# Page numbers loaded four at a time, and reductions, gates, one weight tile and the first weighings moved within their engines' lists, in a one-core decoder step

## The chip, the cores and the metric

The kernel runs on one core of a Trainium2 chip. The metric is the device time of one execution in microseconds (us). Less is better.

## What is computed

One inference step of one decoder layer, for a prompt of 1024 tokens and for eight single new tokens ("samples") with stored state. Four mixers read the same normed input through one input projection `w_in`; their gated outputs go through one output projection. Cut to what matters here:

```python
h = rms_norm(x, norm_pre); proj = h @ w_in              # 1024 x 7688 columns
# A: causal pooling over windows of 2, 4, 8, 16
# B: mLSTM, 4 heads of 128:   num = (q k^T * w_intra) v + (q C) * w_inter
#    C_new = w_old * C + sum_s w_s k_s v_s^T ;  h = num / max(|den|, exp(-m))
# C: stick-breaking attention, 8 heads of 64, strictly causal:
#    A[t,s] = sigmoid(z_ts) * prod_{s<j<t} (1 - sigmoid(z_tj)),  out = A v
#    a sample attends to 4096 stored tokens: 32 pages of 128, by page_table
k_past = cache_sb_k[page_table]; v_past = cache_sb_v[page_table]
# D: softmax cross-attention, 4 heads, into 256 memory tokens
out = rms_norm(concat(A, B, C, D) * gates @ w_out, norm_post); y = x + out
```

## The kernel before

Every engine has its own list, written out by hand; semaphores tie them together, and an engine that waits holds up all that stands behind it in its list. There are five stages, and a stage starts when all engines have left the one before: the first (norm, transposes, memory keys and values, first projections; to about 95 us), stick-breaking (to 500), mLSTM (to 825), memory attention and pooling (to 1134), output projection.

TensorE (PE) multiplies everything. The projections of w_in are done in column tiles of 128: a tile is loaded by SyncE (SP), split into a high half by ScalarE (ACT, `w_hi`) and a low half by VectorE (DVE, `w_lo`), and multiplied in 3 chunks of 24 matmuls (line 417 in the first two stages, line 163 later). A chunk needs both halves. Two tiles' halves are held at a time.

The samples' part of C runs beside this. The 4096 stored tokens are handled in 16 pairs of pages per sample. For keys: SP loads two page numbers into registers (`value_load`, line 2225), waits until the ring of 4 pairs has room (`z_ready`: the pair four before has been reduced) and issues two DMAs (line 2229); GpSimd (POOL) multiplies the pair by the query (line 2237); DVE reduces it to scores (`reduce_keys`, line 2243). After 16 pairs come `add_bias`, a softplus on ACT and DVE (`softplus`, line 2267), a sum on PE (`sum_pages`, line 2275), `exponents` and the weights. For values: SP loads two page numbers and issues two DMAs (lines 2353, 2357) when PE has weighed the pair four before, and PE weighs two pairs at a time (`weigh`, line 2370). Samples 0 to 3 have their keys in the first two stages and their values in stick-breaking; samples 4 to 7 have their keys in mLSTM (one per head) and their values in the memory stage.

Stick-breaking goes in 4 passes `i` of two heads each (called heads here), each of 12 rounds `u`, counted from 0 (HALF is round 4). In a round PE computes scores, one projection chunk, transposes the weights of two rounds ago and weighs the values of three rounds ago (line 1153). DVE does in a round: scans (lines 990, 994), products (line 1003), where due `open_gate`, `split_lo` (line 396), `exponents`, and then `reduce_keys(i + 1, REDUCES[i][u])`. `gate(i, 0)` (line 1010) multiplies the first half of the outputs by the gate; PE's weighing in round 7 writes the same bank and waits for it (`y_taken`). It stands at the start of round 7, behind the reductions of round 6. In the first head `REDUCES[0]` puts the first two reductions of sample 1 in round 2, ahead of `softplus(0)` of sample 0, for which `sum_pages(0)` on PE waits in round 3. SP's list in the first head (lines 814 to 849) has, in this order: key pairs 4 to 8, the values' store, key pair 9, the fourth projection tile (for rounds 9 to 11, split in round 6), key pairs 10 and 11, value pairs 4 and 5, and so on.

mLSTM has four heads with five tiles each: K, V, Q, O, G. In each head SP loads 4 key pairs, then Q, 3 key pairs, the stored C, then O (lines 1783 to 1795). PE multiplies V, transposes K, multiplies Q's first chunk, transposes V (`turn_values`: it needs DVE's `b_kw_tok`, and that needs ACT's `b_w_col`, which stands behind ACT's split of O), then Q's other chunks; `spread_values` (line 2105) waits for DVE's eight updates of C (line 1965).

## Time and profile before

| | |
|---|---|
| median of 3 runs | 1342.79 us (1336.55 to 1345.03) |
| the profiled execution | 1344.1 us; its span 1342.4 us |
| PE busy | 1227.8 us, 91% of the span |
| DVE, ACT, POOL busy | 832.4, 472.1, 388.2 us |
| granted TensorE clock, mean | 0.961 of full speed |
| DMA | 235.80 MB, 176 GB/s on average |

The page gives busy times per engine, the span in 40 slices, the chain of work that ended last and the costliest groups of instructions. A wait is shown as idle time of an engine with what ended it. "SPq" is SyncE's queue, whose register and DMA-issuing instructions are not counted as busy.

### The profile page before, as it was taken

The numbers are of one execution on the slowest core, as the hardware profiler recorded it, in microseconds if no ns is written. First come the engines' busy times: TensorE is split into PE (matmuls) and PEld (weight loads), VectorE is DVE, ScalarE is ACT, GpSimd is POOL, SyncE is SP. The second block draws the span as 40 slices with busy tenths as digits, with TensorE's granted clock in tenths as the row PEclk, the third lists the DMA queues.
The fourth block names the chain that finished last, engine by engine and source line by source line (L and its number), as shares of the span: only waits on it lengthen the run. The fifth ranks groups of instructions, "written<-read, shape, count | busy, mean of one in ns | idle before, by whom it ended". The sixth has DMA issues, their size and how long they took to land.

```text
span 1342.4 us, 22563 instructions
## 1 busy us (share of the span) xinstructions
PE 1227.8 (91%) x7621; PEld 1027.2 (77%) x7621; DVE 832.4 (62%) x1096; ACT 472.1 (35%) x873; POOL 388.2 (29%) x261
## 2 busy tenths in 40 slices
PE   5896989989989986899999999799999998999997
PEld 5885757768768666799998998587888876568886
DVE  5758987999974544779798696343543344433221
ACT  6524535545545741132321324312222132322211
POOL 2476534433530015547664562000000000000000
PEclk9998989999999987899998999899999998999999
DMA  8776488587583446466555542856556654645220
GB/s 287 231 221 189 125 255 248 165 244 226 164 261 105 137 90 212 142 199 203 184 173 181 168 152 87 265 178 196 170 178 203 192 173 141 204 145 171 63 63 32
DMA packets 201029, 235.80 MB, mean 176 GB/s; under 512 B 13763, under 2 KB 122514, under 8 KB 200906
## 3 DMA queue, kind: packets, MB, share of 16 engines
q1 hardware_dynamic: 195282, 218.18, 53.1%
q0 software_dynamic: 5632, 16.18, 3.4%
q8 instruction: 61, 1.00, 0.3%
q14 instruction: 54, 0.44, 0.1%
HBM read 213.78 MB, written 20.63 MB: 175 GB/s over the span
## 4 chain that ended last, share of the span: by engine, by line
PE 52%; DVE 15%; issue 11%; SPq 10%; DMA 7%; ACT 4%; POOL 1%; DVEq 0%; POOLq 0%; ACTq 0%
PE bank L163 15%; PE bank L2665 13%; PE bank L417 7%; PE bank L2370 3%; SPq L2229 3%; SPq L2225 2%; DVE bp_page_z L2243 2%; DMA ring<-w_in 2%; SPq L2353 2%; SPq L2357 1%; PE bank L1120 1%; DVE w_lo L151 1%; PE bank L1153 1%; DVE cp_page_z L2243 1%; PE bank L1637 1%
## 5 line engine op out<-in xcount | busy, mean ns | idle before, releaser
L163 PE MATMUL bank<-xh,w_hi 128*128 128x344 f32 x864 | 290.3, 336 | 12.3 <-DVE w_lo L151 12.0
L163 PE MATMUL bank<-xh,w_lo 128*128 128x344 f32 x864 | 279.5, 323 | 0.0
L163 PE MATMUL bank<-xl,w_hi 128*128 128x344 f32 x864 | 279.4, 323 | 0.0
L2237 POOL TENSOR_TENSOR ring<-ring,cp_q 128x1024 f32<-128x1024 f32 x64 | 165.0, 2599 | 143.7 <-DMA ring<-cache_sb_k 143.5
L2237 POOL TENSOR_TENSOR bp_keys<-bp_keys,bp_q 128x1024 f32<-128x1024 f32 x64 | 169.1, 2661 | 117.7 <-DMA bp_keys<-cache_sb_k 117.5
L163 PEld LDWEIGHTS bank<-xh,w_hi 128*128 128x128 f32 x864 | 166.1, 192 | 43.3 <-issue 28.5
L163 PEld LDWEIGHTS bank<-xl,w_hi 128*128 128x128 f32 x864 | 165.8, 192 | 1.4 <-issue 1.2
L163 PEld LDWEIGHTS bank<-xh,w_lo 128*128 128x128 f32 x864 | 165.5, 192 | 0.0
L417 PE MATMUL bank<-xh,w_hi 128*128 128x344 f32 x408 | 135.0, 331 | 1.7 <-DVE w_lo L396 1.1
L417 PE MATMUL bank<-xh,w_lo 128*128 128x344 f32 x408 | 131.6, 323 | 0.0
L417 PE MATMUL bank<-xl,w_hi 128*128 128x344 f32 x408 | 131.4, 322 | 0.0
L151 DVE TENSOR_TENSOR w_lo<-ring,w_hi 128x1024 fp32r<-128x1024 f32 x36 | 56.6, 1572 | 74.2 <-ACT w_hi L147 74.2
L2665 PE MATMUL bank<-o_w_hi,o_mix_hi 128*128 128x512 f32 x256 | 101.1, 395 | 0.8 <-DVE o_mix_lo L2597 0.6
L2665 PE MATMUL bank<-o_w_hi,o_mix_lo 128*128 128x512 f32 x256 | 99.9, 390 | 0.0
L2665 PE MATMUL bank<-o_w_lo,o_mix_hi 128*128 128x512 f32 x256 | 99.9, 390 | 0.0
L990 DVE TENSOR_TENSOR_SCAN c_left<-c_keep,ones 128x128 f32<-128x128 f32 (+3 forms) x64 | 88.9, 1429 | 14.1 <-ACT c_keep L896 14.1
L1003 DVE TENSOR_TENSOR c_A<-c_A,c_left 128x512 f32<-128x512 f32 (+3 forms) x96 | 78.4, 854 | 21.9 <-ACT c_A L904 21.7
L904 ACT ACTIVATE c_A<-bank,cp_page_bias 128x512 f32<-128x512 f32 (+3 forms) x96 | 51.2, 579 | 111.9 <-PE bank L1138 111.4
L417 PEld LDWEIGHTS bank<-xh,w_hi 128*128 128x128 f32 x408 | 78.2, 192 | 11.9 <-issue 9.6
L2243 DVE TENSOR_REDUCE bp_page_z<-bp_keys 128x16 f32<-128x1024 f32 x64 | 74.9, 1213 | 19.4 <-POOL bp_keys L2237 19.3
L2243 DVE TENSOR_REDUCE cp_page_z<-ring 128x16 f32<-128x1024 f32 x64 | 75.7, 1211 | 13.3 <-POOL ring L2237 13.3
L417 PEld LDWEIGHTS bank<-xl,w_hi 128*128 128x128 f32 x408 | 78.0, 191 | 0.0
(368 smaller groups left out, 2035.3 us busy)
## 6 DMA issues: line engine op xcount, KB each, us to landing
ring<-cache_sb_k SPq DMA_DIRECT2D x128, 256.0 KB, 2.9
cp_values<-cache_sb_v SPq DMA_DIRECT2D x128, 256.0 KB, 3.1
bp_keys<-cache_sb_k SPq DMA_DIRECT2D x128, 256.0 KB, 3.1
dp_values<-cache_sb_v SPq DMA_DIRECT2D x128, 256.0 KB, 2.8
ring<-w_in SPq DMA_DIRECT2D x36, 512.0 KB, 5.9
o_raw<-w_out SPq DMA_DIRECT2D x8, 1024.0 KB, 5.7
c_w_raw<-w_in SPq DMA_DIRECT2D x15, 512.0 KB, 5.1
o_mix<-mix SPq DMA_DIRECT2D x7, 1024.0 KB, 6.7
```

Of the source, the lines that this page charges most:

```text
L151: self.nc.vector.tensor_tensor(self.lo[:, j % 2], self.raw[:, j % 2], self.hi[:, j % 2].bitcast(F32), ALU.subtract).then_inc(self.lo_ready, 1)
L163: last = self.nc.tensor.matmul(self.bank(j, c), w[:, j % 2, k, :], x[:, k, c * CH:(c + 1) * CH], start=(k == 0 and n == 0), stop=(k == KT ...
L417: last = self.nc.tensor.matmul(self.bank(j, c), w[:, k, :], x[:, k, columns], start=(k == 0 and m == 0), stop=(k == KT - 1 and m == 2))
L904: nc.scalar.activation(A[:, n % RA, 0:w], Z[h][:, 0:w], ACT.Sigmoid, bias=bias[:, 2 * i + h:2 * i + h + 1]).then_inc(sig_ready, 1)
L990: nc.vector.tensor_tensor_scan(left[:, n % RL, W - w:W][:, ::-1], keep[:, n % RK, W - w:W][:, ::-1], k.ones512[:, 0:w], 1.0, ALU.mult, ALU ...
L1003: nc.vector.tensor_tensor(A[:, n % RA, 0:w], A[:, n % RA, 0:w], left[:, n % RL, W - w + 1:W + 1], ALU.mult).then_inc(A_ready, 1)
L2225: pages = [queue.value_load(self.page_ids[0:1, page - e:page - e + 1], min_val=0, max_val=self.k.n_phys - 1) for e in range(2)]
L2229: queue.dma_start(self.keys[:, s, e, :], self.k.cache_k[bass.ds(pages[e] * PAGE, PAGE), :]).then_inc(self.K_in[s].sem, 16)
L2237: self.nc.gpsimd.tensor_tensor(self.keys[:, s], self.keys[:, s], q, ALU.mult).then_inc(self.scaled.sem, 1)
L2243: self.nc.vector.tensor_reduce(self.z[:, i % 2, :, 2 * r:2 * r + 2].rearrange("p h r -> p r h"), self.keys[:, r % self.ring].rearrange("p ...
L2370: last = self.nc.tensor.matmul(self.PARTIAL[g:g + SBH, :], self.A[:, i % self.A.shape[1], p, :], self.values[:, t % self.ring, e, :], star ...
L2665: last = nc.tensor.matmul(ACC[b % 3][h][:, :], m[:, b % 2, kk, :], w[:, kk, half(h)], start=first and n == 0, stop=final and n == 2)
```

## The change

1. **Page numbers.** A new class `PageIds` replaces the two `value_load`s per pair: at an even pair one `queue.load` brings four numbers into four registers, for this pair and the next. `value_load` also issued an address operation and an assertion for each number; `snap` does not. It serves keys and values alike.

```diff
+class PageIds:
+    def pair(self, queue, table, sample, r):
+        if (sample, r) not in self.kept:
+            first = sample * NPG + NPG - 2 * (r - r % 2) - 4
+            numbers = [queue.alloc_register(f"{self.tag}_page_{sample}_{r}_{e}") for e in range(4)]
+            queue.load(numbers, table[0:1, first:first + 4])
+            pages = [queue.snap(n, donate=True, min_val=0, max_val=self.k.n_phys - 1) for n in numbers]
+            for e in range(2):
+                self.kept[sample, r - r % 2 + e] = pages[3 - 2 * e], pages[2 - 2 * e]
+        return self.kept.pop((sample, r))
@@ load_keys (load_values alike)
-        page = (i + self.first) * NPG - 2 * r + NPG - 1
-        pages = [queue.value_load(self.page_ids[0:1, page - e:page - e + 1], min_val=0, max_val=self.k.n_phys - 1) for e in range(2)]
+        pages = self.ids.pair(queue, self.page_ids, i + self.first, r)
```

2. **Stick-breaking, DVE.** Sample 1's reductions in the first head start in round 3, and `gate(i, 0)` goes from the start of round 7 to round 6, ahead of the reductions there, in all four heads.

```diff
-    REDUCES = (0, 0, 2, 2, 2, 2, 2, 2, 1, 2, 1, 0), *(...)
+    REDUCES = (0, 0, 0, 2, 2, 2, 2, 2, 2, 2, 2, 0), *(...)
-            if u == HALF + 3:
-                gate(i, 0)
...
+            if u == HALF + 2 and i < GT:
+                gate(i, 0)
             if i < GT:
                 reduce_keys(i + 1, REDUCES[i][u])
```

3. **mLSTM, first head.** Its Q tile is loaded by SP at the end of stick-breaking, and O ahead of key pairs 4 to 6; DVE's reductions come later in its list, the last five behind the low half of the next head's K tile.

```diff
@@ stick-breaking, sync
+        flow.load(sp, 2, k.w_in[:, :, B_Q:B_Q + P])
@@ mLSTM, sync
-            load_tile(i, Q_)
-            load_keys(i, 4, 7)
             if i:
+                load_tile(i, Q_)
+                load_keys(i, 4, 7)
...
             load_tile(i, O_)
+            if i == 0:
+                load_keys(i, 4, 7)
@@ mLSTM, vector (places of reduce_keys in the first head)
-            reduce_keys(i, 0, 4)          # ahead of split Q
-                reduce_keys(i, 4, 7)      # behind split O
+                reduce_keys(i, 0, 3)
-            reduce_keys(i, 7, 11)         # ahead of the updates of C
+            reduce_keys(i, *((7, 11) if i else (3, 6)))
-            reduce_keys(i, 11, 13)        # behind C_new
+            reduce_keys(i, *((11, 13) if i else (6, 9)))
-            reduce_keys(i, 13, paged.PAIRS)
+                reduce_keys(i, 9, 11)
             split(i + 1, K_)
+            if i == 0:
+                reduce_keys(i, 11, paged.PAIRS)
```

4. **Memory stage.** SP issues the load of the page numbers first instead of third, and the four small DMAs of `setup_sync` behind the first four value pairs; PE weighs for the first time before the second chunk of tile 1 instead of the first, and the displaced weighing stands before tile 3.

```diff
-    WEIGHED_FIRST = {(1, 0): 0, (1, 1): 1, (1, 2): 2, (2, 0): 3, (2, 1): 4, (2, 2): 5, (3, 1): 6, (3, 2): 7}
+    WEIGHED_FIRST = {(1, 1): 0, (1, 2): 1, (2, 0): 2, (2, 1): 3, (2, 2): 4, (3, 0): 5, (3, 1): 6, (3, 2): 7}
```

How the lists look now. **DVE, first head of stick-breaking, rounds 2 and 3**, before (`cp_page_L` is the softplus of sample 0, `cp_page_z<-ring` the reductions):

```order
L2252 TENSOR_TENSOR cp_page_z<-cp_page_z,cp_page_bias 128x256
L990 SCALAR_TENSOR_TENSOR c_left<-c_keep,ones 128x384 x2
L1003 TENSOR_TENSOR c_A<-c_A,c_left 128x384 x2
L2243 TENSOR_REDUCE cp_page_z<-ring 128x2x8 x2
L2267 SCALAR_TENSOR_TENSOR cp_page_L<-cp_page_z,cp_page_soft 128x256
L990 SCALAR_TENSOR_TENSOR c_left<-c_keep,ones 128x512 x2
```

and in the change:

```order
L2279 TENSOR_TENSOR cp_page_z<-cp_page_z,cp_page_bias 128x256
L991 SCALAR_TENSOR_TENSOR c_left<-c_keep,ones 128x384 x2
L1004 TENSOR_TENSOR c_A<-c_A,c_left 128x384 x2
L2294 SCALAR_TENSOR_TENSOR cp_page_L<-cp_page_z,cp_page_soft 128x256
L991 SCALAR_TENSOR_TENSOR c_left<-c_keep,ones 128x512 x2
```

The two reductions between the products and the softplus are gone from round 2. **DVE, round 6 and the start of round 7**, before (`mix_cols` 128x512 is the gate):

```order
L990 SCALAR_TENSOR_TENSOR c_left<-c_keep,ones 128x256 x2
L1003 TENSOR_TENSOR c_A<-c_A,c_left 128x256 x2
L396 TENSOR_TENSOR w_lo<-c_w_raw,w_hi 128x1024
L2243 TENSOR_REDUCE cp_page_z<-ring 128x2x8 x2
L1010 TENSOR_TENSOR mix_cols<-bank,mix_cols 128x512
L994 SCALAR_TENSOR_TENSOR c_left<-c_keep,c_left,ones 128x513 x2
```

and in the change:

```order
L991 SCALAR_TENSOR_TENSOR c_left<-c_keep,ones 128x256 x2
L1004 TENSOR_TENSOR c_A<-c_A,c_left 128x256 x2
L396 TENSOR_TENSOR w_lo<-c_w_raw,w_hi 128x1024
L1011 TENSOR_TENSOR mix_cols<-bank,mix_cols 128x512
L2270 TENSOR_REDUCE cp_page_z<-ring 128x2x8 x2
L995 SCALAR_TENSOR_TENSOR c_left<-c_keep,c_left,ones 128x513 x2
```

The gate now stands ahead of the two reductions and directly behind the low half of the fourth tile. These two were the ninth and tenth reductions of sample 1 before and are the seventh and eighth now. **DVE, first head of mLSTM** before, from the head's first sums on (`w_lo` is first that of Q, then that of O):

```order
L1923 TENSOR_TENSOR ring<-b_rows,b_a_col 128x1024
L1926 TENSOR_TENSOR ring<-ring,up_to 128x1024
L2243 TENSOR_REDUCE bp_page_z<-bp_keys 128x2x8 x4
L151 TENSOR_TENSOR w_lo<-ring,w_hi 128x1024
L1941 TENSOR_TENSOR b_kw_tok<-bank,b_w_col 128x512 x2
L1944 TENSOR_TENSOR b_v_diag<-ident,b_vT 128x1024
L1949 COPY b_v_tok<-bank 128x4x128 x2
L151 TENSOR_TENSOR w_lo<-ring,w_hi 128x1024
L2243 TENSOR_REDUCE bp_page_z<-bp_keys 128x2x8 x3
```

and in the change:

```order
L1927 TENSOR_TENSOR ring<-b_rows,b_a_col 128x1024
L1930 TENSOR_TENSOR ring<-ring,up_to 128x1024
L151 TENSOR_TENSOR w_lo<-ring,w_hi 128x1024
L1946 TENSOR_TENSOR b_kw_tok<-bank,b_w_col 128x512 x2
L1949 TENSOR_TENSOR b_v_diag<-ident,b_vT 128x1024
L1954 COPY b_v_tok<-bank 128x4x128 x2
L151 TENSOR_TENSOR w_lo<-ring,w_hi 128x1024
L2270 TENSOR_REDUCE bp_page_z<-bp_keys 128x2x8 x3
```

The four reductions ahead of Q's low half are gone, and three stand behind O's. **SP, the first key pair in mLSTM** before (one pair; ISA rows set addresses and assert):

```order
L2219 DMA bp_q<-new_q 128x512
L2225 TENSOR_LOAD bp_page_ids
L2225 ISA x2
L2225 TENSOR_LOAD bp_page_ids
L2225 ISA x2
L2229 ISA
L2229 DMA bp_keys<-cache_sb_k 128x512
L2229 ISA
L2229 DMA bp_keys<-cache_sb_k 128x512
```

and in the change, two pairs:

```order
L2247 DMA bp_q<-new_q 128x512
L2193 TENSOR_LOAD bp_page_ids
L2256 ISA
L2256 DMA bp_keys<-cache_sb_k 128x512
L2256 ISA
L2256 DMA bp_keys<-cache_sb_k 128x512
L2256 ISA
L2256 DMA bp_keys<-cache_sb_k 128x512
L2256 ISA
L2256 DMA bp_keys<-cache_sb_k 128x512
```

One load of four numbers stands where there were four loads, each with two further rows.

## Rows read from the trace of the kernel before

**Rows 1.** the page: busy us, share of the span, instructions

```profile
PE 1227.8 (91%) x7621; PEld 1027.2 (77%) x7621; DVE 832.4 (62%) x1096; ACT 472.1 (35%) x873; POOL 388.2 (29%) x261
```

**Rows 2.** TensorE's waits, whole run: line, awaited, total us, times, longest

```profile
PE bank L163 <- DVE w_lo L151: 12.0, 1, 12.0
PE bank L2275 <- issue: 10.9, 4, 8.3
PE bank L2370 <- DMA cp_values<-cache_sb_v: 9.7, 5, 3.5
PE bank L2370 <- DMA dp_values<-cache_sb_v: 9.2, 3, 5.3
PE bank L1153 <- DVE mix_cols L1010: 8.5, 4, 4.0
...
PE bank L2105 <- DVE b_C L1965: 4.5, 1, 4.5
PE bank L2157 <- DVE b_C_new L1988: 4.4, 3, 3.1
PE bank L1120 <- SPq L57: 3.1, 1, 3.1
```

**Rows 3.** stretches at half clock: length, PE, PEld, DVE, ACT, POOL busy, PEclk, DMA

```profile
123.80:140.80 17.00, 10.25 (x38) 8.46 (x39) 15.13 (x10) 3.98 (x9) 14.31 (x6) 0.50 0.27 93
168.10:178.30 10.20, 5.60 (x22) 2.45 (x23) 8.99 (x9) 1.59 (x3) 4.32 (x4) 0.50 0.86 266
519.70:533.30 13.60, 6.06 (x21) 6.09 (x22) 5.81 (x4) 3.33 (x7) 10.85 (x5) 0.50 0.85 265
724.50:734.70 10.20, 10.20 (x45) 10.20 (x44) 8.75 (x22) 0.00 (x0) 4.86 (x5) 0.50 0.71 214
857.70:864.40 6.70, 6.26 (x23) 4.58 (x24) 4.13 (x8) 2.27 (x5) 0.00 (x0) 0.50 0.85 263
```

**Rows 4.** line 2225, SyncE: duration in ns, least, median, most; first, last start

```profile
L2225 SPq FUSED_REGOPS  x256: 152/152/187, 47.8 to 796.0; - x128
...
L2225 SPq TENSOR_LOAD <-cp_page_ids x128: 260/269/1099, 47.3 to 386.1; - x128
```

**Rows 5.** SyncE in order of time, start of memory stage: start, length, DMA issues

```profile
835.85 7.69 SPq L2357 DMA_DIRECT2D dp_values<-cache_sb_v  x8
```

**Rows 6.** SyncE in order of time, third head: one pair without its loads

```profile
386.90 0.87 SPq L2229 DMA_DIRECT2D ring<-cache_sb_k  x2
```

**Rows 7.** VectorE in order of time, first head, round 2: start, length

```profile
119.04 1.00 DVE L1003 TENSOR_TENSOR c_A<-c_A,c_left 128x384 f32<-128x384 f32 x2
...
128.02 1.41 DVE L2267 SCALAR_TENSOR_TENSOR cp_page_L<-cp_page_z,cp_page_soft 128x256 f32<-128x256 f32 x1
```

**Rows 8.** VectorE in order of time, first head, rounds 5 to 7

```profile
161.00 2.34 DVE L2243 TENSOR_REDUCE cp_page_z<-ring 128x16 f32<-128x1024 f32 x2
...
168.48 0.68 DVE L1010 TENSOR_TENSOR mix_cols<-bank,mix_cols 128x512 f32<-128x512 f32 x1
```

**Rows 9.** TensorE in order of time, first head, round 7: values waited for

```profile
173.39 1.89 PE L2370 MATMUL bank<-cp_values,c_page_A 128*8 128x512 f32 x8 [3.48 <-DMA cp_values<-cache_sb_v]
```

**Rows 10.** SyncE in order of time, mLSTM's first head: an O tile's issue

```profile
525.82 0.51 SPq L141 DMA_DIRECT2D ring<-w_in  x1
```

**Rows 11.** ScalarE in order of time: that tile's high half

```profile
532.06 1.06 ACT L147 ACTIVATE w_hi<-ring 128x1024 fp32r<-128x1024 f32 x1 [7.62 <-DMA ring<-w_in]
```

**Rows 12.** VectorE in order of time, mLSTM's first head, before Q's low half

```profile
509.00 1.23 DVE L1926 TENSOR_TENSOR ring<-ring,up_to 128x1024 f32<-128x1024 f32 x1
```

**Rows 13.** TensorE in order of time: Q's first chunk begins

```profile
527.24 0.63 PE L163 MATMUL bank<-xh,w_hi 128*128 128x344 f32 x1 [11.95 <-DVE w_lo L151]
```

**Rows 14.** second head of stick-breaking: length, PE, PEld, DVE, ACT, POOL busy

```profile
229.00:328.00 99.00, 91.17 (x664) 71.05 (x663) 94.14 (x82) 52.27 (x101) 43.91 (x19) 0.98 0.71 219
```

**Rows 15.** VectorE by form, 229 to 328 us (GpSimd multiplying pages): busy, mean ns

```profile
L1003 DVE TENSOR_TENSOR c_A<-c_A,c_left 128x512 f32<-128x512 f32 x12 | 13.7, 1180 | 1.1 <-ACT c_A L904 1.1
```

**Rows 16.** the same, 440 to 495 us (GpSimd without pages)

```profile
L1003 DVE TENSOR_TENSOR c_A<-c_A,c_left 128x512 f32<-128x512 f32 x10 | 6.4, 675 | 1.9 <-ACT c_A L904 1.9
```

23 lines of the change are left out of this document (16 added, 7 removed).

## The prediction, made before the changed kernel was run

> **What bounds the kernel now.** I read the page's busy times first: TensorE is busy for 1227.8 us, no other engine for more than 832.4 (VectorE) [rows 1]. The profiled execution took 1344.1 us, 1.3 more than the median of 1342.79; the sum below is made against 1344.1 and 1.3 is taken off at the end. About 116 us remain in which TensorE multiplies nothing. A change that removes no matmul can gain only there, and in the speed of the matmuls. So the second view is TensorE's waits [rows 2]: eight kinds that this change could touch sum to 62.3 us, the two longest single ones 12.0 us (mLSTM's first head, for Q's low half) and 8.3 us (stick-breaking, for the softplus of sample 0). The third is the granted clock: behind the long waits it falls to half, that is to 1.2 of 2.4 GHz, and stays there for 7 to 17 us [rows 3]. In such a stretch the same matmuls would take about half their busy time at the full clock: 10.25/2 = 5.1 us behind the softplus wait, 5.60/2 = 2.8 at round 7, 6.06/2 = 3.0 behind the wait for Q, 10.20/2 = 5.1 in a later mLSTM head, 6.26/2 = 3.1 in the memory stage. A wait thus costs its own length and something behind it, and both go together.
>
> **What a page number costs.** Four pairs of pages need 7.69 us on SyncE from the first DMA issue to the end of the last [rows 5]; one pair without its loads 0.87 [rows 6]. A pair so takes (7.69 - 0.87)/3 = 2.27 us. Of these, 2 x (0.269 + 0.152) = 0.84 us are the two loads and address operations [rows 4]; the other 0.56 are gaps around them and the assertions. Now a pair carries half of one load. If loading four numbers costs what loading one does, a pair takes 0.87 + 0.27/2 and some gaps, about 1.25 us; if it costs four times as much, 1.08 us per load, 1.25 - 0.13 + 0.54 = 1.66. No row shows a load of four. I take 1.25, since what surrounds the two loads (gaps, address operations) goes in either case, and keep 1.66 as a rival.
>
> The Trainium skill ("Runtime: NRT & Kernel Launch", section "Instruction fetch mechanics") says that a register load costs about 200 ns per register even in bulk. That speaks against this change: 0.8 us for a load of four, or 0.4 per pair instead of 0.135. For single loads the trace agrees, 269 ns each; for four it shows nothing. By the page the pair would be near 1.5 us and the time near 1308.
>
> SyncE's speed matters only where TensorE waits for pages or for a tile queued behind them.
>
> **Term a, end of the first stage.** TensorE waits 3.1 us for SyncE to leave the stage (line 1120) [rows 2]; its last work there is key pairs. At 1 us less for each of three or more pairs I take 2.3 (bounds 1.0 and 3.1).
>
> **Term b, first head of stick-breaking.** The products end at 119.04 + 1.00 = 120.04, the softplus starts at 128.02, behind two reductions [rows 7]. With these gone from round 2 it starts 7.98 us earlier, and the 8.3 us wait of `sum_pages` goes to 0.3. Of the clock's 5.1 I take 3.5. That is 11.5. Given back: every reduction of sample 1 is now one round later in number: the pair of reductions that ends at 161.00 + 2.34 = 163.34 [rows 8] is the seventh and eighth before, the fifth and sixth now. SyncE's key pair 9 waits for the sixth (it needs the ring's place of pair 5), and the fourth projection tile is behind it. From 163.34: 1.4 us for pair 9 (1.25 and the wake), 6.2 for the tile (issued at 525.82, in ScalarE's hands at 532.06 [rows 10, 11]), 1.06 for its high half [rows 11], 1.2 for the low half (as long as the 128x1024 operation of 1.23 us [rows 12]), 0.68 for the gate: it ends 10.5 us behind those reductions, where before it ended at 169.16, 5.8 behind them. That gate releases TensorE's weighing, where it waited up to 4.0 us before, and the value pages behind it, waited for until 173.39 [rows 2, 9]. Late next is thus the gate behind the tile, by 4.7 us against VectorE's rhythm; but VectorE is about 8 us earlier, and the pages wait for SyncE, which is cheaper by some 1 us for each of some seven pairs. I count 7.5 given back, so that b nets 4 (bounds 0, all is lost again in rounds 6 and 7, and 13, nothing is).
>
> **Term c, the other heads of stick-breaking.** There the tile is early, and moving the gate ahead of two reductions takes 2.34 us off the waits for it: 8.5 us in four cases, of which the first head's 3.4 to 4.0 stand in b; 2.3 and 0.8 remain. Waits for value pages sum to 9.7, the first head's 3.48 aside 6.2 [rows 2, 9]; there SyncE's list ran without a pause, and I take 5. With b's neighbours in the clock, most of 2.8 [rows 3], 2 are in doubt, and the sum is rounded down to 8 (bounds 3 and 12). The reductions moved behind the gate delay nothing while GpSimd has multiplied ahead.
>
> **Term d, mLSTM's first head.** Q's first chunk begins at 527.24 after a wait of 11.95 [rows 13], so TensorE was ready at 515.29. The tile is now loaded in the stage before, and nothing stands ahead of its low half but the sums that end at 509.00 + 1.23 = 510.23 [rows 12]: it is ready by 511.5 and the wait is gone, with 3.0 of clock [rows 3]: 15. Late next: `turn_values` behind Q's first chunk needs `b_w_col`, which stands behind ScalarE's split of O. SyncE issues O behind four key pairs (5 us at 1.25) and the stored C, near 514.6 by my count; 6.2 for it to land, 1.06 for the high half, 0.9 for the column and VectorE's product: 522.8 to 524. TensorE ends the chunk of 24 matmuls near 519. A new wait of about 4, and 1 of clock, net 10. The wait for the updates of C, 4.5 (line 2105), should lose 4, as seven reductions are no longer ahead of them. d is 14 (bounds 7, where the new wait is 8 and brings the low clock, and 22, where O is in time). The last reductions are behind the low half of K of the second head, and late next is sample 4's sum, which has a head's time.
>
> **Term e, mLSTM's heads 2 to 4.** The waits at line 2157 are 4.4 and the slow stretch at 724.5 could return up to 5.1 [rows 2, 3]. What changes there is SyncE alone: three pairs ahead of O are 1 us each cheaper. I take 4 (bounds 0 and 9).
>
> **Term f, memory stage.** Waits of 9.2 us for value pages [rows 2] and 3.1 of clock [rows 3]. The first page numbers go out first, pairs are 1 us cheaper, and TensorE weighs one chunk later (3 to 4 us, 24 matmuls). All 12.3 should go, but late next is tile 2, behind them on SyncE, and the weighings moved on: less 4, gives 8 (bounds 4 and 12).
>
> **Sum.** 2.3 + 4 + 8 + 14 + 4 + 8 = 40.3. 1344.1 - 40.3 - 1.3 = 1302.5 us. All lower bounds sum to 15 (1327.8), all upper ones to 71 (1271.8). Since the terms are in different stages, they will not all fall to one side: likeliest case 1293 to 1314.
>
> **The rivals.**
> - *Waits come back* (18%). The fourth tile, the value pages and mLSTM's O tile are each behind something new. If b nets 0, c 5, d 7, e 0 and f 6 beside a's 2.3, the gain is 20 to 22: 1321. For it: three of the six terms have a named successor. Against it: the successors are all on SyncE, which becomes almost twice as fast.
> - *A load of four costs four* (12%). The 0.41 us more per pair times the 12 to 15 pairs on which TensorE really waits is 6: 1309. This is the Trainium skill's rule quoted above, whose own figure gives nearly the same.
> - *Everything closes and the clock comes back in full* (10%). About 60 of the 71: 1284.
> - *The change does nothing* (6%): other engines are ready no earlier, and each wait passes on to ScalarE or POOL: 1342.
> - *The other side: VectorE becomes the bound* (4%). In the second head VectorE is busy 94.14 of 99.00 us [rows 14]. Its 128x512 products take 1180 ns while GpSimd multiplies pages and 675 when it doesn't [rows 15, 16]. A faster SyncE bunches GpSimd's 19 operations of 43.91 us [rows 14] onto VectorE's. If all 48 scans and products of a pass (12 rounds, two of each) were slowed by that difference, 0.505 us, VectorE would have 24 us more per pass; less 5 us of slack, in three heads, 57. 1342.8 - 41 + 57 = 1358. It decides from where VectorE lengthens by more than 5 + 41/3 = 19 us per pass. Against it: most of these products are slowed already. The Trainium skill ("SBUF — State Buffer", section "SBUF: two separate sides") has the two engines exclude each other at the port for such operations; by that rule the overlap is paid whenever it falls, and the trace agrees, at 1.7 times the duration, but GpSimd's total work is unchanged.
>
> **How the numbers follow.** The likeliest case has 50%. A measurement of this kernel can tell about 1% from no change, 13.4 us. The range leaves out "nothing" and "the other side" (10%) and most of the 1284 case (10%): 1288 to 1322, with about 80% inside. Faster than 1329.4: the forecast and the first three rivals (90%) less a share of the first for its upper edge, 0.88; within 1%: 0.08; slower: 0.04.
>
> **What would show it.** Page numbers: SyncE's period of four pairs near 5 us instead of 7.69, and the duration of the load (0.27 against 1.08). b: line 2275's first wait under 1 us; the wait for the gate in round 7 of the first head, and what ScalarE waits for before the fourth tile's high half. c: the waits for value pages near 1 in all. d: no wait for Q's low half near 515; a new one of about 4 us behind the first chunk, released by `b_kw_tok`; line 2105's at 0.5. e: the clock at 724. f: no wait for the values of the memory stage, and a wait for tile 2's halves instead. Other side: VectorE's mean for the 128x512 product over 1.2 us and its busy share at 99% in the second head. The forecast is wrong if the new waits of b and d are each over 8 us, or if the clock falls in places where it was full before.

## The result

| | before | changed |
|---|---|---|
| median of 4 runs each, us | 1340.73 (1336.55 to 1345.03) | 1327.01 (1323.86 to 1327.79) |
| changed to before, 95% interval | | 0.9893 (0.9867 to 0.992) |
| the profiled execution: span, us | 1342.4 | 1322.1 |
| TensorE busy, us | 1227.8 | 1212.6 |
| VectorE busy, us | 832.4 | 823.5 |
| granted TensorE clock, mean | 0.961 | 0.969 |

The change gains 1.1%, some 14 us by the medians; the forecast of 1302.5 us lies 38 below the same median. The profiled execution of before was near the slow end of its runs and that of the change is its fastest, so the two traces lie 20.3 us apart. The prediction's sum was made against the trace of before, so in the traces its 40.3 stands against these 20.3. The page's busy times and TensorE's waits of the changed kernel (line, awaited, total us, times, longest):

```profile
PE 1212.6 (92%) x7621; PEld 1018.9 (77%) x7621; DVE 823.5 (62%) x1096; ACT 471.7 (36%) x873; POOL 389.7 (29%) x261
```

```profile
PE bank L2302 <- issue: 20.4, 3, 11.3
...
PE bank L2397 <- DMA cp_values<-cache_sb_v: 10.7, 2, 10.5
PE bank L1154 <- DVE mix_cols L1011: 8.6, 2, 7.9
PE bank L2103 <- DVE b_kw_tok L1946: 7.1, 1, 7.1
...
PE bank L163 <- ACT mix_cols L179: 4.1, 1, 4.1
PE bank L2130 <- ACT b_sq L1867: 3.8, 2, 2.7
...
PE bank L417 <- DVE w_lo L396: 3.0, 1, 3.0
```

Against [rows 2]: the wait for Q's low half (12.0), those for the memory stage's values (9.2), for the updates of C (4.5), at old line 2157 (4.4) and for SyncE (3.1) are gone. But the samples' sum (old line 2275, now 2302) has 20.4 us instead of 10.9 and two long waits instead of one; a single wait for value pages is 10.5 us; the gate is waited for 7.9 us at once; new are 7.1 us for `b_kw_tok` and 4.1 for ScalarE at the start of the memory stage. The waits shown above sum to 57.7 us, the eight of [rows 2] to 62.3: most of what closed came back elsewhere.

Where TensorE gains and loses shows best on single matmuls. All projections stand in one order in both kernels, so the same matmul can be looked up in both traces. Its start, and what TensorE gained since the row above:

| matmul starts, before | changed | ahead (+) by | gained since | part |
|---|---|---|---|---|
| 20.7 | 20.7 | 0.0 | | |
| 100.9 | 102.2 | -1.3 | -1.3 | first stage (term a: +2.3) |
| 161.2 | 158.9 | +2.3 | +3.6 | to round 5 (b) |
| 181.3 | 191.1 | -9.8 | -12.1 | rounds 6 and 7 (b: +4 in all) |
| 498.0 | 495.0 | +3.0 | +12.8 | other heads (c: +8) |
| 572.2 | 555.1 | +17.1 | +14.1 | mLSTM's first head (d: +14) |
| 612.5 | 612.5 | 0.0 | -17.1 | start of the second head |
| 818.7 | 806.8 | +11.8 | +11.8 | heads 2 to 4 (e: +4) |
| 929.3 | 909.2 | +20.1 | +8.3 | memory stage (f: +8) |
| 1305.4 | 1285.2 | +20.2 | +0.1 | the rest |

Two places lose 29 us together: rounds 6 and 7 of the first head, where the forecast had counted 7.5 given back, and the start of mLSTM's second head, where it had nothing. Both have a half-clock stretch behind the wait (stretches of the changed kernel: length, busy us of PE, PEld, DVE, ACT, POOL, then the granted clock, the DMA share and GB/s):

```profile
127.40:134.20 6.80, 3.53 (x12) 2.36 (x12) 5.72 (x5) 1.32 (x3) 2.59 (x1) 0.50 0.00 0
168.40:188.90 20.50, 6.96 (x26) 3.81 (x27) 11.62 (x12) 5.74 (x10) 9.39 (x5) 0.50 0.70 242
588.20:601.90 13.70, 5.13 (x16) 4.80 (x17) 13.63 (x9) 1.06 (x1) 9.02 (x5) 0.50 0.29 98
```

The first is shorter than that at 123.80 in [rows 3], the second is 20.5 us where 10.2 were, the third is new.

**The page numbers** cost what the prediction took. Line 2193 on SyncE (ns: least, median, most), and four pairs of keys from the first issue to the last's end:

```profile
L2193 SPq TENSOR_LOAD <-cp_page_ids x64: 293/302/969, 48.6 to 468.2; - x64
L2193 SPq TENSOR_LOAD <-bp_page_ids x32: 293/302/1072, 505.9 to 778.1; - x32
```

```profile
115.54 4.60 SPq L2256 DMA_DIRECT2D ring<-cache_sb_k  x8
```

The row at 115.54 holds eight DMA issues, two for each pair. A load of four takes 302 ns where a load of one took 269 [rows 4], and a pair (4.60 - 0.87)/3 = 1.24 us against 1.25 forecast and 2.27 before [rows 5].

### The profile page after: what moved, and what is told of

It is laid out like the page before. It is cut to its first block, busy times and chain, and to the rows that moved or that the text cites. A ratio compares the mean times of both kernels' runs of the same rounds, so it can differ in the third digit from the quotient of the medians.

```text
span 1322.1 us, 21155 instructions
## 1 busy us (share of the span) xinstructions
PE 1212.6 (92%) x7621; PEld 1018.9 (77%) x7621; DVE 823.5 (62%) x1096; ACT 471.7 (36%) x873; POOL 389.7 (29%) x261
## 4 chain that ended last, share of the span: by engine, by line
PE 74%; issue 8%; DMA 6%; DVE 4%; ACT 4%; SPq 2%; PEld 1%; DVEq 0%; POOLq 0%; POOL 0%; ACTq 0%; PEldq 0%
PE bank L163 26%; PE bank L417 13%; PE bank L2692 13%; PE bank L2397 4%; DMA ring<-w_in 2%; PE bank L1121 2%; PE bank L1154 2%; PE bank L1139 2%; PE bank L1639 1%; PE bank L1690 1%; ACT L114 1%; PE bank L1622 1%; PE bank L2706 1%; PE bank L1696 1%; SPq L2256 1%
## 5 line engine op out<-in xcount | busy, mean ns | idle before, releaser
L2264 POOL TENSOR_TENSOR ring<-ring,cp_q 128x1024 f32<-128x1024 f32 x64 | 166.2, 2616 | 140.3 <-DMA ring<-cache_sb_k 140.2
L2264 POOL TENSOR_TENSOR bp_keys<-bp_keys,bp_q 128x1024 f32<-128x1024 f32 x64 | 169.3, 2666 | 111.0 <-DMA bp_keys<-cache_sb_k 110.8
L163 PEld LDWEIGHTS bank<-xh,w_lo 128*128 128x128 f32 x864 | 164.2, 190 | 0.0
L151 DVE TENSOR_TENSOR w_lo<-ring,w_hi 128x1024 fp32r<-128x1024 f32 x36 | 51.6, 1433 | 67.2 <-ACT w_hi L147 67.2
L417 PEld LDWEIGHTS bank<-xh,w_hi 128*128 128x128 f32 x408 | 77.8, 191 | 13.1 <-issue 11.6
L1004 DVE TENSOR_TENSOR c_A<-c_A,c_left 128x512 f32<-128x512 f32 (+3 forms) x96 | 72.4, 791 | 18.2 <-ACT c_A L905 18.0
L417 PEld LDWEIGHTS bank<-xh,w_lo 128*128 128x128 f32 x408 | 77.6, 190 | 0.0
```

Source lines behind the costliest of these rows:

```text
L151: self.nc.vector.tensor_tensor(self.lo[:, j % 2], self.raw[:, j % 2], self.hi[:, j % 2].bitcast(F32), ALU.subtract).then_inc(self.lo_ready, 1)
L163: last = self.nc.tensor.matmul(self.bank(j, c), w[:, j % 2, k, :], x[:, k, c * CH:(c + 1) * CH], start=(k == 0 and n == 0), stop=(k == KT ...
L417: last = self.nc.tensor.matmul(self.bank(j, c), w[:, k, :], x[:, k, columns], start=(k == 0 and m == 0), stop=(k == KT - 1 and m == 2))
L1004: nc.vector.tensor_tensor(A[:, n % RA, 0:w], A[:, n % RA, 0:w], left[:, n % RL, W - w + 1:W + 1], ALU.mult).then_inc(A_ready, 1)
L2264: self.nc.gpsimd.tensor_tensor(self.keys[:, s], self.keys[:, s], q, ALU.mult).then_inc(self.scaled.sem, 1)
```

## The experiments

Each kernel was timed beside the kernel before on the same chip; ratios are to it, with 95% intervals.

| kernel | median us | ratio to before |
|---|---|---|
| the change | 1327.01 | 0.9893 (0.9867 to 0.992) |
| ids_only | 1329.42 | 0.9879 (0.9834 to 0.9924) |
| lists_only | 1346.08 | 1.0029 (1.0002 to 1.0056) |
| old_reduces | 1316.89 | 0.9813 (0.9776 to 0.985) |
| hold_keys | 1323.49 | 0.984 (0.9804 to 0.9875) |
| early_hold | 1319.27 | 0.9842 (0.9801 to 0.9883) |
| mlstm_hold | 1333.57 | 0.995 (0.9927 to 0.9973) |
| mlstm_tile | 1314.39 | 0.9829 (0.9777 to 0.9881) |
| halves | 1303.76 | 0.9728 (0.9697 to 0.976) |
| change_halves | 1315.13 | 0.9825 (0.9776 to 0.9874) |
| before_halves | 1323.82 | 0.9893 (0.9849 to 0.9938) |
| halves_tile | 1300.48 | 0.972 (0.9675 to 0.9765) |
| halves_no3 | 1299.07 | 0.9714 (0.9672 to 0.9755) |
| no_part3 | 1319.7 | 0.9837 (0.9783 to 0.9891) |
| gate_in_round7 | 1325.25 | 0.9887 (0.9848 to 0.9926) |
| sum_early | 1305.74 | 0.9726 (0.967 to 0.9781) |
| no_part4 | 1323.55 | 0.9858 (0.9794 to 0.9922) |

Where intervals overlap, I go by the two traces, matmul against matmul as in the table above, and say so; the times of a stretch are then those of the kernel compared with. One trace is one execution, and how far a gain can be trusted depends on the place. Here is what TensorE gained on the trace of before in the traces of all kernels that have the same lists in that stretch (GpSimd's multiplications undivided, the page numbers by four):

| stretch of before | kernels | least to most | mean | forecast |
|---|---|---|---|---|
| to 100.9, term a | 10 | -1.9 to +3.7 | +0.6 | +2.3 |
| 161.2 to 181.3, reductions a round later | 2 | -12.1 to -11.3 | -11.7 | |
| the same, reductions as before | 8 | +0.3 to +1.9 | +1.2 | |
| 181.3 to 498.0, term c | 8 | +5.6 to +12.8 | +8.3 | +8 |
| 498.0 to 572.2, with part 3 | 8 | +13.1 to +14.6 | +13.7 | +14 (term d) |
| 572.2 to 612.5, with part 3 | 6 | -17.1 to -7.5 | -13.2 | |
| 612.5 to 818.7, term e | 9 | -1.4 to +11.8 | +4.7 | +4 |
| 818.7 to 929.3, term f, with part 4 | 8 | +4.0 to +8.4 | +6.0 | +8 |

The loss in rounds 6 and 7 comes back in both traces with late reductions, the gain of the first mLSTM head and the loss in the second in every trace with part 3; a difference of a few us in terms a, c, e or f does not.

### Which part of the change gains: ids_only and lists_only

ids_only puts `PageIds` and its two calls into the kernel before. lists_only takes them out of the changed kernel, so that each pair again has two `value_load`s:

```diff
-        pages = self.ids.pair(queue, self.page_ids, i + self.first, r)
+        page = (i + self.first) * NPG - 2 * r + NPG - 1
+        pages = [queue.value_load(self.page_ids[0:1, page - e:page - e + 1], ...) for e in range(2)]
```

> The kernel before with the page numbers loaded by four and nothing else. Theory (SyncE's faster pairs help where TensorE waits for pages, but bunch GpSimd's multiplications onto VectorE's operations with two SBUF inputs): the waits for the memory stage's values drop from 9.2 us to below 5, mLSTM's wait for Q's low half from 12 to 8 or 10, and the softplus of sample 0 comes no earlier than before although its two reductions can start about 3 us earlier. Time between 1325 and 1334. Rival (the loads alone carry the whole gain of the change, the moved lists nothing): 1327 or less. Rival (a faster SyncE is worth nothing by itself): 1338 to 1342.

> The changed kernel with the page numbers loaded one by one as before. Theory: VectorE's two slow products in the round of the softplus disappear, since GpSimd starts about 3 us later again (its multiplications then start behind the products), so line 2302's first wait drops from 7.8 to below 4 us; the fourth projection tile and the value pages in rounds 6 and 7 are as late as in the changed kernel or later; the memory stage's waits return in part. Time between 1328 and 1340. Rival (the moves alone are what slows VectorE, whatever SyncE's speed): the products take 5.2 us here too and the wait stays near 8.

The loads alone carry the whole measured gain (0.9879 against 0.9893); the time, 1329.42, is in the range of the theory, and the rival for 1327 or less missed by 2 us. Two of the theory's waits came out too long: 6.5 us for the memory stage's values (below 5 expected) and 11.0 us for Q's low half (8 to 10 expected). The moved lists alone gain nothing (1.0029). So something in parts 2 to 4 loses (the theory had 1328 to 1340 for it, too good) as much as their good steps gain. In lists_only VectorE's two products of round 2 take 1.00 us as expected and the long wait at the sum is gone, but the value pages are waited for 13.1 us at once:

```profile
PE bank L2399 <- DMA cp_values<-cache_sb_v: 21.3, 6, 13.1
```

An earlier softplus is thus not enough, and the loss in rounds 6 and 7 doesn't need the faster SyncE.

### Reductions a round later: old_reduces

```diff
-    REDUCES = (0, 0, 0, 2, 2, 2, 2, 2, 2, 2, 2, 0)
+    REDUCES = (0, 0, 2, 2, 2, 2, 2, 2, 1, 2, 1, 0)
```

> The changed kernel with the first row of REDUCES as before: two reductions of sample 1 in round 2 again, each later one back a round earlier. Theory (the loss of 12 us between 161 and 191 us comes from reductions that are a round later and hold up key pair 9, the fourth projection tile and value pages 4 and 5 on SyncE): the wait for the value pages in round 7 falls from 10.5 to below 4 us, the gate's wait from 7.9 to below 4, and the time is 8 to 13 us below the changed kernel: about 1316. Rival (the gate ahead of the reductions is what delays the value pages): those waits stay above 14 us in sum and the time is within 3 us of the changed kernel. The softplus wait should be 6 to 10 us in either case.

```profile
PE bank L2302 <- issue: 22.1, 4, 11.2
...
PE bank L2397 <- DMA cp_values<-cache_sb_v: 5.0, 3, 4.6
...
PE bank L1154 <- DVE mix_cols L1011: 3.9, 3, 2.4
```

The value pages' wait fell from 10.5 to 4.6 us (below 4 expected), the gate's from 7.9 to 2.4, and the time is 0.8% below the change's, with separate intervals; between 161.2 and 181.3 us of before TensorE gains 0.5 where the change lost 12.1. The softplus wait stays at 7.9 us, with its reductions in front or not. The rival (the gate) is out. Up to the gate the chain is the one that the prediction named: the changed kernel's ScalarE gets the fourth tile only at 168.50, 11.40 us after it last worked, while that of old_reduces has it at 155.52 without a wait:

```profile
168.50 1.06 ACT L391 ACTIVATE w_hi<-c_w_raw 128x1024 fp32r<-128x1024 f32 x1 [11.40 <-DMA c_w_raw<-w_in]
```

The chain has one more link, on SyncE. Between the fourth tile and value pairs 4 and 5 stand key pairs 10 and 11, and they wait for the seventh and eighth reductions. Before, these were those of round 5; in the change they are those of round 6, and they now stand behind the tile's low half and the gate. SyncE before, then in the change:

```profile
162.50 3.56 SPq L2229 DMA_DIRECT2D ring<-cache_sb_k  x4
167.43 3.11 SPq L2357 DMA_DIRECT2D cp_values<-cache_sb_v  x4
```

```profile
172.79 2.06 SPq L2256 DMA_DIRECT2D ring<-cache_sb_k  x4
175.45 1.98 SPq L2384 DMA_DIRECT2D cp_values<-cache_sb_v  x4
```

The value pages are issued 8.0 us later than before, though the pairs ahead of them are cheaper; in old_reduces they are issued at 162.62.

### What holds the softplus: hold_keys and early_hold

Without the two reductions the softplus of sample 0 was to start at 120; in the changed kernel it starts at 127.72. VectorE (start, length), and GpSimd's multiplications at the same time:

```profile
118.68 3.95 DVE L991 TENSOR_TENSOR_SCAN c_left<-c_keep,ones 128x384 f32<-128x384 f32 x2
122.55 5.24 DVE L1004 TENSOR_TENSOR c_A<-c_A,c_left 128x384 f32<-128x384 f32 x2
127.72 2.56 DVE L2294 SCALAR_TENSOR_TENSOR cp_page_L<-cp_page_z,cp_page_soft 128x256 f32<-128x256 f32 x1
```

```profile
119.06 10.93 POOL L2264 TENSOR_TENSOR ring<-ring,cp_q 128x1024 f32<-128x1024 f32 x4 [8.59 <-DMA ring<-cache_sb_k]
```

The two products take 5.24 us, where the same two took 1.00 before [rows 7]. hold_keys moves GpSimd:

```diff
+                if i == 0 and r == 0:
+                    pool.wait_ge(keys.L_ready.sem, keys.L_ready.at(0, 1))
                 if i + 1 < GT:
                     keys.multiply_keys(pool, i + 1, r)
```

> The changed kernel with one wait added on GpSimd: sample 1's first key pair is multiplied only when VectorE has written the softplus of sample 0. Nothing else changes. Theory (VectorE's two products and the softplus, 5.2 and 2.6 us here against 1.0 and 0.4 alone, are held up by GpSimd's multiplications): the two 128x384 scans take 1.8 us, the products 1.0, the softplus 0.4, it ends near 122 us, and line 2302's first wait falls from 7.8 to below 1 us; later operations of VectorE in round 3 take the collisions instead. Rival (the operations are slow for another reason, such as transfers into the same memory): durations stay and the wait grows or stays at 8 us. Time: 3 to 9 us below the changed kernel by the theory, unchanged or above by the rival.

```profile
118.53 1.80 DVE L991 TENSOR_TENSOR_SCAN c_left<-c_keep,ones 128x384 f32<-128x384 f32 x2
120.25 1.00 DVE L1004 TENSOR_TENSOR c_A<-c_A,c_left 128x384 f32<-128x384 f32 x2
...
122.55 5.80 DVE L991 TENSOR_TENSOR_SCAN c_left<-c_keep,ones 128x512 f32<-128x512 f32 x2 [0.97 <-ACT c_keep L897]
128.27 5.58 DVE L1004 TENSOR_TENSOR c_A<-c_A,c_left 128x512 f32<-128x512 f32 x2
```

```profile
121.66 11.64 POOL L2266 TENSOR_TENSOR ring<-ring,cp_q 128x1024 f32<-128x1024 f32 x4 [11.34 <-DVE cp_page_L L2296]
```

Scans 1.80, products 1.00, and TensorE does not wait at that sum any more: VectorE was held up by GpSimd, and the next scans and products, now beside the four multiplications, take 5.80 and 5.58 us instead. At 141 us of before TensorE is 11.4 us ahead (the change: 2.1), and 11.3 are lost again between 161.2 and 181.3: the value pages come when SyncE may issue them, not when TensorE arrives. The time is not measurably another than the change's (0.984 and 0.9893 overlap); the theory held for the durations and the wait, and the total (3.5 us lower by the medians, 3 to 9 expected) doesn't tell.

early_hold puts both together: REDUCES as before, the softplus in front of round 2's reductions, and the hold.

```diff
+            if g == 2:
+                keys.softplus(dve, 0)
             if i < GT:
                 reduce_keys(i + 1, REDUCES[i][u])
```

> The kernel old_reduces (the change, with REDUCES as before) and two edits: in round 2 of the first head VectorE does the softplus of sample 0 ahead of the two reductions, and GpSimd multiplies sample 1's first key pair only behind that softplus, as in hold_keys. Theory: it joins what hold_keys and old_reduces each gained. Line 2302's first wait is below 1 us, the value pages wait 5 us or less, and TensorE is 6 to 9 us ahead of old_reduces at 140 us; of that 3 to 8 remain at 200 us. Time 1309 to 1314. Rival (what the softplus gains is taken back by rounds 6 and 7 in any case, since the fourth tile and the value pages are set by GpSimd's pace and not by TensorE): ahead at 140, level with old_reduces at 200, time 1315 to 1319.

The rival holds: 4.9 us gained on old_reduces between 110.8 and 142.5 us, 4.7 of it given back by 173.4; total 0.9842 against 0.9813, no difference that can be measured. The wait for the softplus, the second longest of the kernel before, is worth nothing by itself.

### Taking turns: halves, change_halves, before_halves

```diff
-        q = self.q[:].rearrange("p (o c) -> p o c", o=1).to_broadcast([P, 2, GW])
-        self.nc.gpsimd.tensor_tensor(self.keys[:, s], self.keys[:, s], q, ALU.mult).then_inc(self.scaled.sem, 1)
+        for e in range(2):
+            last = self.nc.gpsimd.tensor_tensor(self.keys[:, s, e], self.keys[:, s, e], self.q[:], ALU.mult)
+        last.then_inc(self.scaled.sem, 1)
```

> The kernel old_reduces with each multiplication of a key pair on GpSimd split into two of 128x512, one page each; nothing is left out. Theory (a VectorE operation with two SBUF inputs waits for the GpSimd operation that is running, and GpSimd then waits for it: each is held up by one whole operation of the other): in round 2 of the first head the two scans and the two products, 3.96 and 5.24 us for a pair, fall to about 2.9 and 3.1, since what is waited for is half as long; the first wait of line 2302 falls from 7.9 to 4 or 5; in the second mLSTM head the wait falls from 11.2 to 7 or 8. Time 2 to 8 us below old_reduces. Rival (the slowing is shared bandwidth, not taking turns): VectorE's operations take as long as with whole pairs. GpSimd itself may need up to 10% longer for two operations than for one.

```profile
115.88 2.85 DVE L991 TENSOR_TENSOR_SCAN c_left<-c_keep,ones 128x384 f32<-128x384 f32 x2
118.65 3.10 DVE L1004 TENSOR_TENSOR c_A<-c_A,c_left 128x384 f32<-128x384 f32 x2
...
124.05 0.41 DVE L2295 SCALAR_TENSOR_TENSOR cp_page_L<-cp_page_z,cp_page_soft 128x256 f32<-128x256 f32 x1
```

```profile
116.24 13.64 POOL L2264 TENSOR_TENSOR ring<-ring,cp_q 128x512 f32<-128x512 f32 x8 [7.03 <-DMA ring<-cache_sb_k]
```

Twice as many operations, each half as long: the scans beside them take 2.85 us and the products 3.10 (forecast 2.9 and 3.1), the wait at the sum 4.8. By the rival, shared bandwidth, they would have stayed as long as with whole pairs. halves is 0.9% below old_reduces, with separate intervals, for an edit that makes GpSimd's own work longer (mean 1536 ns twice for a pair of samples 0 to 3, 2616 ns once in the changed kernel). By the medians that is 13 us, more than the 2 to 8 that the theory had.

> The changed kernel, with its late reductions, and each multiplication of a key pair on GpSimd split into two of one page each. Theory (the two engines take turns, operation by operation, and halving GpSimd's operations halves each hold-up of VectorE; in the kernel old_reduces this gave 13 us): 9 to 14 us below the changed kernel, 1313 to 1318; the sum's first wait 4 to 5 us, but the waits for the fourth tile's gate and for the value pages in round 7 stay above 12 us in sum, since they come from reductions a round later. Rival (the split helped only where the reductions were early): within 4 us of the changed kernel.

> The kernel before with GpSimd's multiplications split in two and nothing else: the control for change_halves. Theory (the hold-ups cost before too, since VectorE's products take 1.18 us in the second head against 0.68 alone, but less, as SyncE's slower pairs leave gaps between GpSimd's multiplications): 3 to 9 us below the kernel before, 1332 to 1338. If the gain is 10 us or more, the hold-ups were as dear before as after, and the change's missing gain is not theirs. If it is none, they matter only with the faster SyncE.

change_halves came out as expected: 1315, with 6.0 us for the gate and 10.0 for the value pages left. The control did not: the split gives the kernel before 1.07%, 13 to 14 us (8 to 20 by the interval), more than the 3 to 9 of the theory and no less than it gives the change (0.7%, 9 to 12 us). By the sentence on record, taking turns was as dear before as after. It explains why single waits did not close, not why the change's total is 24 us short.

### mLSTM's second head: mlstm_hold, mlstm_tile, sum_early

In the changed kernel TensorE reaches the sum of sample 4 at 585.4 and waits until 596.8. VectorE ahead of the softplus, and GpSimd:

```profile
584.25 3.29 DVE L1930 TENSOR_TENSOR ring<-ring,up_to 128x1024 f32<-128x1024 f32 x1
587.46 3.37 DVE L1904 SCALAR_TENSOR_TENSOR b_ln<-b_h,b_gain_all,b_ln 128x1032 f32<-128x1032 f32 x1
590.87 3.25 DVE L1908 TENSOR_TENSOR mix_cols<-mix_cols,b_ln 128x1032 f32<-128x1032 f32 x1
594.15 2.19 DVE L1910 COPY new_mix<-mix_cols 128x8 f32<-128x8 f32 x1
596.26 0.41 DVE L2294 SCALAR_TENSOR_TENSOR bp_page_L<-bp_page_z,bp_page_soft 128x256 f32<-128x256 f32 x1
```

```profile
583.57 12.75 POOL L2264 TENSOR_TENSOR bp_keys<-bp_keys,bp_q 128x1024 f32<-128x1024 f32 x4 [7.76 <-DMA bp_keys<-cache_sb_k]
```

Three operations of 1.2 to 1.3 us and a copy of 0.17 us (their durations in mlstm_hold) take 12 us in all beside four multiplications. The V tile that VectorE splits just before was issued on SyncE at 569.08 behind key pairs and reached ScalarE at 580.68:

```profile
569.08 0.39 SPq L141 DMA_DIRECT2D ring<-w_in  x1
```

```profile
580.68 1.06 ACT L147 ACTIVATE w_hi<-ring 128x1024 fp32r<-128x1024 f32 x1 [6.09 <-DMA ring<-w_in]
```

mlstm_hold (on old_reduces) lets GpSimd start a sample only behind the softplus of the one before; mlstm_tile (on old_reduces) issues that tile earlier:

```diff
+                if r == 0 and i:
+                    pool.wait_ge(paged.L_ready.sem, paged.L_ready.at(i - 1, 1))
                 paged.multiply_keys(pool, i, r)
```

```diff
+            if i == 0:
+                load_tile(i + 1, V_)
             load_keys(i, 13, paged.PAIRS)
             load_rows(i + 1)
-            load_tile(i + 1, V_)
+            if i:
+                load_tile(i + 1, V_)
```

> The kernel old_reduces with one more wait on GpSimd in mLSTM: a sample's first key pair is multiplied only behind the softplus of the sample before it (heads 2 to 4). Theory (in the second head GpSimd's four multiplications hold up VectorE's four long operations ahead of the softplus, 3.2 to 3.4 us each against 1.2 to 1.3 alone): these take 1.2 to 1.3 us, the softplus comes 6 to 8 us earlier, line 2302's longest wait falls from 11.2 to 3 to 5 us, the half-clock stretch behind it shrinks, and the time is 5 to 10 us below old_reduces. Rival (the wait comes from the late tile of V alone, which VectorE splits at 581 us): VectorE's operations are as slow or the wait falls by less than 2 us.

> The kernel old_reduces with V's tile of the second mLSTM head issued on SyncE ahead of key pairs 13 to 15 and of the gate rows, where it stood behind them. Theory (the tile's landing, 11.5 us from its issue in the changed kernel against 6 for other tiles, and its place behind pairs that wait for late reductions, cost 4 to 5 us of line 2302's longest wait; the rest is VectorE's operations held up by GpSimd): ScalarE's high half of that tile starts 4 us or more earlier and the wait falls from 11.2 to 6 to 8 us. Time 3 to 5 us below old_reduces. Rival (the sum is late for the reductions and the rows, not for the tile): the wait stays at 10 us or more.

With the hold the operations take 1.2 to 1.3 us and the wait is 4.9 us instead of 11.2; but behind it stands a new one in each of three heads, 17.1 us in sum, and the kernel is slower than old_reduces by 1.4%. How much of the 6 us the hold took away is not certain: in the six traces with the same lists there and nothing else changed, that wait is 5.1 to 13.1 us (5.1 in no_part4). With the early tile the wait at the sum is gone and TensorE gains 11.4 us on old_reduces between 545.7 and 586.5; 8.8 of that are lost by 616.5, at a wait of 7.4 us for VectorE, which is held up for a whole row of multiplications:

```profile
583.88 7.53 DVE L151 TENSOR_TENSOR w_lo<-ring,w_hi 128x1024 fp32r<-128x1024 f32 x1
```

```profile
583.29 7.03 POOL L2267 TENSOR_TENSOR bp_keys<-bp_keys,bp_q 128x1024 f32<-128x1024 f32 x3
```

Here VectorE did not get its turn between the three multiplications. This is the new wait of mlstm_hold too: the same operation takes 7.53, 7.55 and 7.53 us in its three heads, at 588.32, 671.32 and 751.25, and TensorE's waits of 5.3, 4.9 and 6.9 us follow. halves_tile has it with 7.92 us (TensorE waits 6.4), no_part4 with 5.25, halves with 5.53. It isn't confined to this place. In the 18 traces 48 operations of VectorE take more than 4.5 us, two of them in stick-breaking in every kernel, that before included; VectorE's scans and GpSimd's row there:

```profile
237.10 11.73 DVE L990 TENSOR_TENSOR_SCAN c_left<-c_keep,ones 128x512 f32<-128x512 f32 x2
```

```profile
238.39 9.34 POOL L2237 TENSOR_TENSOR ring<-ring,cp_q 128x1024 f32<-128x1024 f32 x4
```

The second of these scans takes 10.60 us, until the fourth multiplication is over. In all 48 cases the row of multiplications follows within 0.03 us on a DMA issue by GpSimd, the store `mix<-mix_cols`. The reverse does not hold: where VectorE's operation started 0.7 us or more into such a row, the two took turns as elsewhere, and once (before, at 275) one that had started just ahead of the row wasn't held up. No operation outside these 48 takes more than 3.5 us. Splitting doesn't help here (11.16 us beside eight halves). No run moves that store, so what the DMA issue has to do with it isn't shown.

sum_early (on halves) moves the first head's reductions forward in VectorE's list, 3, 4, 4 and 5 of them, all ahead of the next K's low half:

```diff
-            reduce_keys(i, *((7, 11) if i else (3, 6)))
+            reduce_keys(i, *((7, 11) if i else (3, 7)))
...
-            reduce_keys(i, *((11, 13) if i else (6, 9)))
+            reduce_keys(i, *((11, 13) if i else (7, 11)))
...
-                reduce_keys(i, 9, 11)
+            reduce_keys(i, 13 if i else 11, paged.PAIRS)
+            paged.add_bias(dve, i)
```

> The kernel halves with the reductions of mLSTM's first head moved earlier in VectorE's list: 3, 4, 4 and 5 instead of 3, 3, 3, 2 and 5, so that all and the bias stand ahead of the next K's low half, as before the change; Q's and O's tiles are loaded early as in the change. Theory (the sum of sample 4 was late since its last five reductions, behind K's low half, hold up on SyncE the last key pairs, the gate rows and V's tile): V's tile is issued 4 us or more earlier, the wait for the sum falls from 7.9 to below 4, and the time is 3 to 6 us below halves: 1297 to 1301. Rival (the reductions ahead of h's products hold up the square sums instead): a wait of 3 us or more for the squares, time 1302 or more.

```profile
PE bank L2124 <- ACT b_sq L1867: 12.1, 2, 11.0
```

The rival came: the sum's wait is gone and the square sums wait 11.0 us, since h's products stand behind the last five reductions. Of three edits, two remove the wait and one shortens it, and each finds others next to it: twice VectorE shut out behind GpSimd's row, once the square sums.

### What the third part is worth: halves_no3 and no_part3

Both take all of part 3 back (Q's early load, O ahead of the pairs, the places of the reductions), halves_no3 from halves, no_part3 from old_reduces.

> The kernel halves with the change's third part undone: mLSTM's first head has its lists as before (Q's tile behind four key pairs, reductions ahead of Q's low half, none behind the next K's). Theory (part 3 trades the wait for Q's low half, 12 us and its slow clock, for a new wait for V's transposes, 6 us, and for the late sum of sample 4, 8 us): TensorE is 8 to 14 us behind the kernel halves at 540 us and within 4 us of it at 620; time 1302 to 1308. Rival (part 3 is worth the 14 us that were forecast for it): 1314 or more.

> The change with REDUCES as before and its third part (mLSTM's first head) undone: what is left is the page numbers, the gates in round 6 and the memory stage. Theory (part 3 is worth nothing net with undivided multiplications either, as halves_no3 showed with divided ones): 1311 to 1319, within 4 us of the kernel old_reduces; TensorE waits about 11 us for Q's low half again and under 3 for sample 4's sum. Rival (part 3 brings the forecast 14 us here): 1325 or more.

```profile
PE bank L163 <- DVE w_lo L151: 11.3, 1, 11.3
```

Without part 3 the old wait of 11 to 12 us for Q's low half is back and the time is the same: 0.9714 against 0.9728, and 0.9837 against 0.9813, inside the intervals (no_part3's 1319.7 is 0.7 us above its range). In the traces no_part3 loses 10.2 us to old_reduces between 485.1 and 545.7, and has 12.2 back by 586.5. halves_tile, the kernel halves with the early tile, says the same:

> The kernel halves (the change with REDUCES as before and the split multiplications) with V's tile of the second mLSTM head issued ahead of key pairs 13 to 15, as in mlstm_tile. Theory (the tile's part of the sum's wait is its own, apart from the hold-ups; what mlstm_tile lost again was VectorE's low half of Q, which waited 6.3 us while GpSimd did three multiplications in a row): the wait of 7.9 us for the sum falls below 4, 3 to 5 us are gained at 590 us, and at least half of them stays at 620, since the row of multiplications is shorter for each: 1299 to 1302. Rival (the gain passes to the next wait in full): ahead at 590, level at 620, 1303 or more.

Between 543.9 and 576.3 us it gains 6.35 us on halves, and by 606.4 has given 6.5 back: the rival's course; that the time lies in the theory's range says nothing, since by the ratios it is that of halves (0.972 and 0.9728). halves_no3 came out below its range of 1302 to 1308; it loses 11.1 us to halves between 485.0 and 543.9 and has 11.8 back by 606.4, as expected. The three are one time, 1299 to 1304.

### The gates and the memory stage: gate_in_round7 and no_part4

gate_in_round7 (on old_reduces) puts `gate(i, 0)` back to the start of round 7; no_part4 (on old_reduces) takes part 4 back as in the diff ahead.

> The kernel old_reduces with the gate at the start of round 7 again in all four heads. Theory (moving it ahead of two reductions is worth at most 2.3 us in the first head and less in the others, where a faster SyncE leaves little to wait for): waits for the gate up by 1 to 4 us in sum, time 0 to 4 us above old_reduces. Rival (the gate's move carries the gain of 11 us that the other heads of stick-breaking showed): 8 us or more above.

> The kernel old_reduces with the fourth part (memory stage) undone, so that only the loads by four work on its waits. Theory (part 4 carries about half of the 8 us that the memory stage gained): waits for values of 4 to 6 us come back in the memory stage's first tiles, time 2 to 6 us above old_reduces. Rival (the loads by four carry all of it): within 1.5 us.

```profile
PE bank L1154 <- DVE mix_cols L1011: 6.9, 4, 3.4
```

```profile
PE bank L2396 <- DMA dp_values<-cache_sb_v: 5.6, 2, 3.0
```

The gate in round 7 costs 0.7% (the intervals touch); in the traces 7.7 us between 142.5 and 447.6. The waits for it are up by only 3.0 us (6.9 against 3.9), so most of the gate's worth is not in its own waits. Some of it is in the clock: between 142 and 457 us gate_in_round7 is at half clock for 20.4 us, old_reduces for 10.2, and the difference costs up to 5.1; but no_part3 and no_part4, whose gate is in round 6, have 17.0 and 13.6 there, so this isn't the gate's alone. The theory of 0 to 4 us fell, and the rival of 8 or more is nearer. Part 4 is worth 7.9 us in the memory stage by these two traces (801.6 to 895.7), and 5 by the means (6.0 with it, 1.2 without it in no_part4 and ids_only), most of what the stage gained; the waits that come back are 5.6 us, as expected, the total (0.9858 against 0.9813) can't be told apart.

## Why the prediction was wrong

**What a page number costs: right.** 1.24 us per pair for 1.25, and the load of four 0.30 us, so the rival with four times the price is out, and with it the Trainium skill's 0.8 us that stood beside it; the measurement decides. (The skill's page speaks of registers loaded from HBM; these numbers come from a tile in SBUF. And the estimate that stood beside it was high: 0.27 us more on each of 12 to 15 pairs is 1306, not 1308.) Its effect on the total was larger than its share in the sum: alone it carries the measured gain.

**Term a: small, and not told by one trace.** The wait for SyncE (3.1) is gone, but a wait of 3.0 for a low half stands earlier in the stage, with a half-clock stretch behind it; -1.3 instead of +2.3. Ten kernels with the same lists there have -1.9 to +3.7 and a wait of 0.8 to 3.0, so the term is likely under the forecast (mean 0.6); why the wait varies is not shown.

**Term b: wrong, the first failed step.** "With these gone from round 2 it starts 7.98 us earlier" assumed that VectorE's operations take in the new place what they took in the old. They were short before since GpSimd's multiplications began at 122.22, just behind them; a faster SyncE and the missing reductions put them side by side, and hold_keys showed that this is the cause. GpSimd before:

```profile
122.22 15.89 POOL L2237 TENSOR_TENSOR ring<-ring,cp_q 128x1024 f32<-128x1024 f32 x6 [13.11 <-DMA ring<-cache_sb_k]
```

So TensorE gained 3.6 us between 100.9 and 161.2, not 11.5 with the clock; hold_keys had gained 12.5 by 141. The second step, what rounds 6 and 7 give back, named the chain up to the gate (reductions a round later, pair 9, the fourth tile) and timed it well: 10.5 us from the reductions' end to the gate's, 11.1 measured (160.31 to 171.41). It failed in two places. VectorE was to be about 8 us early and was 3.0 early (160.31 for 163.34). And the value pages were to wait only for a cheaper SyncE, while ahead of them key pairs 10 and 11 waited for the reductions behind that gate: issued at 175.45 for 167.43. Sized at 7.5, it measured 12.1, with a slow stretch of 20.5 us in it. Net -8.5 instead of +4, outside the bounds of 0 and 13: a lower bound of "all is lost again" was no bound, since the pages can be later than before.

**Term c: right.** 12.8 for 8 in this trace, 8.3 in the mean of eight. The gate's move is worth more than the 3 us counted for it (gate_in_round7 is 7.7 behind by 447.6).

**Term d: right in its own head, wrong in sum.** +14.1 by 572 us, with the wait of 7.1 for `b_kw_tok` where 4 were forecast. The failed step is its last sentence, that sample 4's sum "has a head's time". It has not: TensorE waits 11.3 us for it, with V's tile late on SyncE and VectorE held up by GpSimd ahead of the softplus, and all 17.1 us that it was ahead were gone again at 612.5. The first head and what follows it thus gave back as much as they had gained, and without part 3 the time is the same (two pairs of kernels).

**Term e: 11.8 for 4 in this trace**, the waits at old line 2157 and the slow stretch at 724.5 [rows 2, 3] both gone; nine kernels with the same lists have -1.4 to +11.8, mean 4.7, so the size was right and the 11.8 largely this execution's. **Term f: 8.3 for 8**, 6.0 in the mean of eight.

**The total.** The measured 1327.01 is near the 1327.8 of all lower bounds, by chance: b fell 8.5 below its lower bound of nothing and d's gain was lost, while c, e and f came out above theirs. Of the two signs that the prediction set for being wrong, half clock where it was full before appeared (at 588); of the new waits, b's was over 8 us (10.5 for value pages), d's named one was 7.1, and the one it had not named, at the sum, 11.3.

**The rivals.** "Waits come back" was what happened, with 1321 forecast for it and 18%; it was also too small, since it took the lower bounds of b and d as floors. The mechanism of "the other side" (VectorE held up by GpSimd) was at work, but local: in the second head of stick-breaking, where it was placed, VectorE's 128x512 products took 1030 ns instead of 1180 [rows 15], its 128x513 scans 2271 instead of 1537; it was busy for 97.77 of 99 us (229 to 328), close to the sign that the prediction had set for this rival, and the heads as a whole gained all the same. The Trainium skill ("SBUF — State Buffer", section "SBUF: two separate sides") says that a VectorE operation with two inputs in SBUF and a GpSimd operation that reads SBUF exclude each other for a whole operation, whichever starts first; I had used it for an average over a head, where it changes nothing, and not for the five operations ahead of the softplus, where it decides. The runs agree with it as far as one operation goes: 1.00 us for two products becomes 5.24 beside whole pairs and 3.10 beside halves. The 48 operations that were shut out for a whole row, some of them started 0.06 to 0.16 us before the row's first multiplication, go beyond it.

**What stays open.** Why the gain of mLSTM's first head is always lost in the second. In mlstm_hold, mlstm_tile and halves_tile the next wait is VectorE's low half of Q, shut out behind GpSimd's row; whether it would be gone with that store elsewhere, no run tests. In the change itself, and in sum_early, the wait is another. It may be that the key work of sample 4 had used TensorE's 12 us wait for Q and has no other room; that is a guess.

**The best version** is none of the two: halves_no3, 1299.07 us, 0.9714 of before (the page numbers, the gates in round 6, the memory stage, the split multiplications, without the late reductions and part 3). halves_tile and halves can't be told from it.

## What to carry to other kernels

- Where a step is moved, take its duration from what other engines do in the new place, not from its row in the old one. Two-input operations of VectorE beside GpSimd's are the case to look for: count the GpSimd operations that will run there, each holds up one, and look for a row of them right behind a DMA issue, which can hold up one operation to its end.
- Before counting the removal of a long wait, list what comes next and who sets its time (reductions, page loads, the order of SyncE's list); here two removed waits of 8 and 12 us were worth nothing net.
- One trace of each kernel doesn't size a term of a few us: with the same lists a stage came out -1.4 to +11.8 us. The means of several kernels do.
- The lower bound of a term whose steps are moved later is not nothing: the thing released last can be later than it ever was. Splitting a long operation of a side engine in two was worth as much on the kernel before (13 us) as the whole change (14).

## What the runs showed of the hardware

- GpSimd and VectorE mostly take turns by operation. Beside multiplications of 2.4 us a VectorE operation with two SBUF inputs ended about 2 us late, whatever its size (the softplus: 0.42 in hold_keys, 2.56 beside them; a 128x1024 sum: 1.22 and 3.29), and so did a 128x8 copy with one input (0.17 and 2.19); GpSimd's own grew from 2.4 to 2.7 or 3.2 us each. Reductions of the same buffers keep 1.21 us throughout.
- The turn isn't sure: 48 VectorE operations in 18 traces took 5.2 to 11.2 us, most of them until a whole undisturbed row of GpSimd's was over (7.53 us beside three multiplications of 7.03 in all, 10.60 beside four of 9.34). Every such row followed directly on a DMA issue by GpSimd.
- Two multiplications of 128x512 kept GpSimd busy for 3.0 to 3.1 us, one of 128x1024 for 2.6 to 2.7, and the kernel was faster with the two.
- A register load of four numbers took 302 ns in the median, of one 269: three further numbers in one load cost 33 ns together.
